# A transformer pair on one core: heads of the first mixer woven into its projections, and two edits to the expert stages

## The reference, cut to what matters

```
p = rms_norm(x) @ w_in            # columns: q,k | v | rg | mq,mk | mv | mo | i,f
y_ret = head_norm(retention(rope(q), rope(k), v)) * silu(rg)       # 4 heads, 64/128 wide
q2, k2 = silu(causal_conv(mq,mk)) # 4 taps
y_ml  = head_norm(gated_attention(q2, k2, mv, gates i and f)) * sigmoid(mo)
x = x + concat(y_ret, y_ml) @ w_out
```

```
expert = top 2 of one group per token;  out = sum_k gate_k * (silu(x @ w1[e]) * (x @ w3[e])) @ w2[e]
```

## Time and profile before

| | us |
|---|---|
| median of three runs (2335.35 to 2337.67) | 2337.12 |
| the profiled execution, its own time | 2344.5 |
| its span | 2342.7 |
| VectorE's wait for the large constants ends | 28.15 |
| first product of the mixer: start, end | 15.72, 31.7 |
| first half of the out product ends (the first out tile free) | 160.7 |
| last out product ends, embedding product begins | 175.76 |
| feed-forward stage begins | 183.6 |
| first weights of expert stage one issued | 1076.2 |
| last hidden product of stage one, of stage two | 1611.4, 2311.4 |

### The profile page before, as it was taken

The page is one execution under the profiler, slowest core; times in us unless marked ns, Lnnn a source line. Parts: engine busy times, 40 slices in busy tenths (PEclk is TensorE's granted clock), DMA queues, the critical chain, the costliest instruction groups (busy, mean ns, idle before and its releaser), DMA issues.

```text
span 2342.7 us, 20745 instructions
## 1 busy us (share of the span) xinstructions
PE 2050.2 (88%) x8573; PEld 1091.0 (47%) x8573; DVE 709.2 (30%) x1346; ACT 343.8 (15%) x725; POOL 65.2 (3%) x79
## 2 busy tenths in 40 slices
PE   7989999998999999999987778785799797887875
PEld 3557776455577764445633333332355433333331
DVE  1247465325475654023300000000764200000001
ACT  1221000214310012000100000001243100000001
POOL 0000000001000000000000000001000000000000
PEclk9979999997999999999899999998799799999998
DMA  8517667344176675112999999999211999999995
GB/s 310 184 36 262 241 216 270 130 169 144 57 267 216 245 270 168 39 72 77 368 428 427 427 427 428 427 428 396 90 56 43 375 428 426 427 429 426 428 427 229
DMA packets 154559, 639.16 MB, mean 273 GB/s; under 512 B 16600, under 2 KB 67480, under 8 KB 129760
## 3 DMA queue, kind: packets, MB, share of 16 engines
q1 hardware_dynamic: 135328, 596.04, 64.1%
q0 software_dynamic: 9824, 24.89, 3.0%
q10 hardware_dynamic: 9312, 16.88, 1.9%
HBM read 622.33 MB, written 25.30 MB: 276 GB/s over the span
## 4 chain that ended last, share of the span: by engine, by line
PE 75%; DMA 13%; issue 6%; DVE 4%; ACT 2%; POOL 0%; SPq 0%; ACTq 0%; DVEq 0%; POOLq 0%
PE psum L492 17%; PE psum L1996 16%; PE psum L934 13%; PE psum L2014 8%; PE psum L909 5%; DMA normed_t<-in_w 4%; DMA ring<-in_w 4%; PE psum L1512 4%; DMA arena<-in_w 1%; PE psum L922 1%; PE psum L1969 1%; DMA expert_inputs<-arena 1%; PE psum L478 1%; PE psum L1645 1%; PE psum L1653 1%
## 5 line engine op out<-in xcount | busy, mean ns | idle before, releaser
L492 PE MATMUL psum<-ring,normed_t 128*128 128x512 f32 (+1 forms) x864 | 355.1, 572 | 6.3 <-DVE scaled L2206 2.5
L934 PE MATMUL psum<-normed_t,ring 128*128 128x256 f32 x1408 | 305.5, 379 | 0.0
L934 PEld LDWEIGHTS psum<-normed_t,ring 128*128 128x128 f32 x1408 | 267.5, 190 | 40.6 <-issue 4.3
L492 PEld LDWEIGHTS psum<-ring,normed_t 128*128 128x128 f32 x864 | 162.1, 199 | 188.2 <-issue 185.2
L1996 PE MATMUL psum<-ring,arena 128*64 128x512 f32 x640 | 196.8, 677 | 51.9 <-issue 51.8
L1996 PE MATMUL psum<-ring,consts 128*64 128x512 f32 x640 | 188.1, 650 | 55.0 <-issue 55.0
L2305 DVE TENSOR_TENSOR scaled<-scaled,psum 128x512 f32<-128x512 f32 x32 | 22.0, 687 | 610.7 <-PE psum L1996 610.7
L839 DVE SCALAR_TENSOR_TENSOR arena<-ring,silu_c,arena 128x1024 f32<-128x1024 f32 x168 | 204.5, 1278 | 0.0
L2014 PE MATMUL psum<-ring,consts 128*64 128x512 f32 x640 | 169.8, 594 | 26.0 <-ACT consts L2144 12.5
L1996 PEld LDWEIGHTS psum<-ring,arena 128*64 128x64 f32 x640 | 65.3, 155 | 178.6 <-issue 178.6
L1996 PEld LDWEIGHTS psum<-ring,consts 128*64 128x64 f32 x640 | 62.3, 148 | 174.4 <-issue 173.8
(11 more groups left out here) (394 smaller groups left out, 2039.9 us busy)
## 6 DMA issues: line engine op xcount, KB each, us to landing
ring<-in_w SPq DMA_DIRECT2D x120, 2048.0 KB, 28.8
arena<-in_w SPq DMA_DIRECT2D x48, 2048.0 KB, 29.3
ring<-in_w_mod SPq DMA_DIRECT2D x24, 2048.0 KB, 8.7
normed_t<-in_w SPq DMA_DIRECT2D x24, 2048.0 KB, 32.8
ring<-in_ffn_w_up SPq DMA_DIRECT2D x44, 1024.0 KB, 9.6
ring<-in_ffn_w_down SPq DMA_DIRECT2D x10, 2048.0 KB, 8.7
expert_outputs<-consts ACTq DMA_DIRECT2D x64, 256.0 KB, 10.7
ring<-in_ab_w_in SPq DMA_DIRECT2D x6, 2048.0 KB, 20.4
```

Of the source, the lines that this page charges most:

```text
L492: m = te.eng.matmul(PS[:, bank, 0:n], src[:, k0 + k, P * t:P * t + P], w[:, k, :], start=(k == 0), stop=(k == kc - 1))
L934: m = pe.matmul(PS[:, b, 256 * hf:256 * hf + 256], w[:, hf, k, P * cc:P * cc + P], HT[:, k, 0:T], start=(k == 0), stop=(k == KC - 1))
```

## The change

1. The gates' tile comes third in the stream, mqk second. The gates are one product of eight rows; a small product with eight columns of the identity (`forget_rows`) moves rows 4 to 7 to a place of their own.
2. The heads of both mixers are cut into steps that `group` and `out_half` put between the projections' products: v carries the gates' second half, rg the retention, mv and mo the second mixer and the turns of the first; the out product is split into its input halves j = 0 and j = 1, so that the first half of all four results comes ahead of the last turns. Banks are dealt anew; ScalarE's and VectorE's lists follow.
3. `Experts.pe` waits for banks 0 to 3 before the picking, not for all.
4. In stage two, for pair 0, the out product goes ahead of the turn of pair 1.

```diff
-        AB_TILES = [("qk", 0, 512), ("v", 512, 512), ("rg", 1024, 512), ("mqk", 1536, 512),
-                    ("mv", 2048, 512), ("mo", 2560, 512), ("if", 3072, 8)]
+        AB_TILES = [("qk", 0, 512), ("mqk", 1536, 512), ("if", 3072, 8), ("v", 512, 512), ("rg", 1024, 512),
+                    ("mv", 2048, 512), ("mo", 2560, 512)]
...
-            for t in range(2):
-                rows(te, "ab.v", t, 2 + t, ("act", f"ab.v{t}"), last=t == 1)
-            for t in range(2):
-                rows(te, "ab.rg", t, 4 + t, ("act", f"ab.rg{t}"), last=t == 1)
...
+
+            w = te.weights("ab.if")[:, 0:64].rearrange("p (k n) -> p k n", k=8)
+            te.take(2, "act", "ab.f")
+            for k in range(KC):
+                m = pe.matmul(PS[0:8, 2, 0:256], w[:, k, :], HT[:, k, 0:T], start=(k == 0), stop=(k == KC - 1))
+            p.step(m, "ab.if.done", "ab.if.used")
...
-            for t in range(2):
-                rows(te, "ab.mv", t, 2 + t, ("dve", f"ab.mv{t}"), last=t == 1)
...
+            def group(name, t, bank, reader, steps):
+                w = te.weights(name).rearrange("p (k n) -> p k n", k=KC)
+                te.take(bank, *reader)
                 for k in range(KC):
-                    m = pe.matmul(PS[0:4, 6, 256 * j:256 * j + 256], w[:, k, 4 * j:4 * j + 4], HT[:, k, 0:T],
-                                  start=(k == 0), stop=(k == KC - 1))
-            p.step(m, "ab.if.done", "ab.if.used")
+                    for step in steps.get(k, ()):
+                        step()
+                    m = pe.matmul(PS[:, bank, :], HT[:, k, P * t:P * t + P], w[:, k, :], start=(k == 0), stop=(k == KC - 1))
+                p.step(m, f"{name}.t{t}", *([f"{name}.used"] if t else []))
+
+            def forget_rows():
+                pe.wait_ge(sems["act"], upto("act", "ab.i"))
+                p.step(pe.matmul(PS[0:4, 2, 256:512], ident[0:8, 4:8], G8, start=True, stop=True), "ab.fsel")
...
+                p.step(m, f"ab.ytr{j}{t}")
+
+            def out_half(n, t, b, j, steps):
+                w = te.weights(f"ab.out{n}").rearrange("p (k n) -> p k n", k=KC)
+                if j == 0:
+                    te.take(b, "dve", f"ab.res{n}{t}")
+                for k in range(4 * j, 4 * j + 4):
+                    for step in steps.get(k, ()):
+                        step()
+                    m = pe.matmul(PS[:, b, :], YH[:, k, P * t:P * t + P], w[:, k, :], start=(k == 0), stop=(k == KC - 1))
+                if j == 1:
+                    p.step(m, f"ab.out{n}.t{t}", *([f"ab.out{n}.used"] if t else []))
+
+            group("ab.v", 0, 3, ("act", "ab.v0"), {2: [forget_rows]})
+            group("ab.v", 1, 4, ("act", "ab.v1"), {})
+            group("ab.rg", 0, 5, ("act", "ab.rg0"), {0: [lambda: ret_scores(0), lambda: ret_scores(1)], 2: [gate_columns],
+                                                     4: [lambda: ret_values(0), lambda: ret_scores(2)],
+                                                     6: [lambda: ret_values(1), lambda: ret_scores(3)]})
+            group("ab.rg", 1, 2, ("act", "ab.rg1"), {1: [lambda: ret_values(2)], 3: [lambda: ret_values(3)]})
+            group("ab.mv", 0, 3, ("dve", "ab.mv0"), {})
+            group("ab.mv", 1, 4, ("dve", "ab.mv1"), {0: [lambda: ml_scores(0)], 4: [lambda: mixed_turn(0, 0, 5), lambda: mixed_turn(0, 1, 2)],
+                                                     6: [lambda: ml_scores(1)]})
+            group("ab.mo", 0, 5, ("act", "ab.mo0"), {2: [lambda: ml_values(0)], 3: [lambda: ml_scores(2)], 6: [lambda: ml_values(1)],
+                                                     7: [lambda: ml_scores(3)]})
+            group("ab.mo", 1, 2, ("act", "ab.mo1"), {3: [lambda: ml_values(2)], 6: [lambda: ml_values(3)]})
+            pe.wait_ge(sems["dve"], upto("dve", "ab.yt01"))
+            out_half(0, 0, 0, 0, {})
+            out_half(1, 0, 1, 0, {})
+            out_half(0, 1, 5, 0, {})
+            out_half(1, 1, 2, 0, {2: [lambda: mixed_turn(1, 0, 3)]})
+            mixed_turn(1, 1, 4)
+            pe.wait_ge(sems["dve"], upto("dve", "ab.yt10"))
+            out_half(0, 0, 0, 1, {})
+            out_half(1, 0, 1, 1, {4: [lambda: emb_turn(te, 0)]})
             pe.wait_ge(sems["dve"], upto("dve", "ab.yt11"))
-            for n in range(2):
-                for t in range(2):
-                    rows(te, f"ab.out{n}", t, 2 * n + t, ("dve", f"ab.res{n}{t}"), src=YH, last=t == 1,
-                         within={(1, 0): (0, lambda: emb_turn(te, 0)), (1, 1): (5, lambda: norm_pe(te, "n.ffn0", (0,)))}.get((n, t), (-1, None)))
+            out_half(0, 1, 5, 1, {})
+            out_half(1, 1, 2, 1, {6: [lambda: norm_pe(te, "n.ffn0", (0,))]})
...
+            for t in range(2):
+                ac.wait_ge(sems["pe"], upto("pe", f"ab.v.t{t}"))
+                p.step(ac.activation(V[:, t, :], PS[:, 3 + t, :], ACT.Copy), f"ab.v{t}")
+                if t == 0:
+                    for c in range(4):
+                        ac.wait_ge(sems["dve"], upto("dve", f"ml.conv{c}"))
+                        p.step(ac.activation(MQK[:, c, :], RTMP[:, c, :], ACT.Silu), f"ml.mqk{c}")
+            for t in range(2):
+                ac.wait_ge(sems["pe"], upto("pe", f"ab.rg.t{t}"))
+                p.step(ac.activation(SRG[:, t, :], PS[:, (5, 2)[t], :], ACT.Silu), f"ab.rg{t}")
             ac.wait_ge(sems["pe"], upto("pe", "ret.pv3"))
             p.settle()
...
+            for t in range(2):
+                ac.wait_ge(sems["pe"], upto("pe", f"ab.mo.t{t}"))
+                p.step(ac.activation(SMO[:, t, :], PS[:, (5, 2)[t], :], ACT.Sigmoid), f"ab.mo{t}")
...
+            head_norm_sums(dv, p, "ret")
+            head_norm_apply(dv, p, "ret", lambda t: PS[:, 6 + t, :], lambda t: SRG[:, t, :], lambda t: YTOK[:, t, 0:512], "ab.y0")
+            values_in(0)
+            g_max(0)
+            ml_causal(0)
+            mixer_columns(0)
+            g_max(1)
+            ml_causal(1)
+            ml_weight(0)
+            values_in(1)
+            ml_weight(1)
+            g_max(2)
+            ml_causal(2)
+            g_max(3)
+            ml_causal(3)
+            ml_weight(2)
+            ml_weight(3)
+            dv.wait_ge(sems["pe"], upto("pe", "ml.pv3"))
+            dv.wait_ge(sems["act"], upto("act", "ml.em"))
...
+            for t in range(2):
+                for n in range(2):
                     if (n, t) == (1, 1):
                         norm_columns(dv, p, "n.ffn0", (0,), lambda t: g_ffn[0])
-                        dv.wait_ge(sems["pe"], upto("pe", "ab.out1.t1"))
-                    p.step(dv.tensor_tensor(xr, xr, PS[:, 2 * n + t, :], ALU.add), f"ab.res{n}{t}")
-                    if n and on("ffn0"):
-                        norm_scale(dv, p, "n.ffn0", t)
+                    dv.wait_ge(sems["pe"], upto("pe", f"ab.out{n}.t{t}"))
+                    xr = X[:, t, 512 * n:512 * n + 512]
+                    p.step(dv.tensor_tensor(xr, xr, PS[:, ((0, 1), (5, 2))[t][n], :], ALU.add), f"ab.res{n}{t}")
+                norm_scale(dv, p, "n.ffn0", t)
...
-                for who in te.banks.values():
-                    wait(pe, *who)
+                for b in range(4):
+                    wait(pe, *te.banks[b])
+                self.pe_first(te)
                 te.banks = {}
-                self.pe_first(te)
...
@@ -2074,9 +2119,12 @@
                 for c in range(PAIRS):
                     self.pe_hidden(te, c, 0)
                     self.pe_hidden(te, c, 1)
-                    if c + 1 < PAIRS:
+                    late = self.nt == 2 and c == 0
+                    if c + 1 < PAIRS and not late:
                         self.pe_turn(te, c + 1)
                     self.pe_out(te, c)
+                    if late:
+                        self.pe_turn(te, 1)
```

More of the change, by code:

```diff
@@ L559, in ab_pe @@
-            pe.wait_ge(sems["dve"], upto("dve", "ml.rows"))
-            pe.wait_ge(consts_loaded, 16)
-            te.take(3, "dve", "ml.cols")
-            for t in range(2):
-                pe.transpose(PS[:, 3, 4 * t:4 * t + 4], gates4[:, 0 + P * t:P * t + P], ident[0:4, 0:4])
-                m = pe.transpose(PS[:, 3, 8 + 4 * t:12 + 4 * t], gates4[:, 256 + P * t:256 + P * t + P], ident[0:4, 0:4])
-            p.step(m, "ml.colt")
-            pe.wait_ge(sems["dve"], upto("dve", "ml.mqk"))
@@ new lines, in gate_columns, with ml_scores @@
+            def gate_columns():
+                pe.wait_ge(sems["dve"], upto("dve", "ml.rows"))
+                te.take(4, "dve", "ml.cols")
+                for t in range(2):
+                    pe.transpose(PS[:, 4, 4 * t:4 * t + 4], gates4[:, 0 + P * t:P * t + P], ident[0:4, 0:4])
+                    m = pe.transpose(PS[:, 4, 8 + 4 * t:12 + 4 * t], gates4[:, 256 + P * t:256 + P * t + P], ident[0:4, 0:4])
+                p.step(m, "ml.colt")
+            def ml_scores(h):
+                if h == 0:
+                    pe.wait_ge(sems["act"], upto("act", "ml.mqk3"))
+                    pe.wait_ge(consts_loaded, 16)
```

(3 more changed lines are left out.)

166 lines of the change are left out of this document (66 added, 100 removed).

## The result

| | median us | runs | profiled execution, us (span, mean clock) |
|---|---|---|---|
| before | 2337.39 | 2335.35, 2337.12, 2337.67, 2343.37 | 2344.5 (2342.7, 0.940) |
| after | 2312.34 | 2309.21, 2311.30, 2313.37, 2315.61 | 2309.21 (2307.4, 0.948) |

Ratio 0.9889, interval 0.9866 to 0.9912: 25.0 us, or 1.1%, faster. The forecast was 2305.5, in a range of 2299 to 2316. The two profiled executions differ by 35.3 us, 10 more than the medians: the one of before was 7 slower than its median, the one of after was the fastest of its four. So what follows compares stages, not whole spans.

What follows compares the result with a forecast made beforehand. TensorE's stream was taken to bound the kernel outside the expert stages, the weight stream within them; -24.5 - 2.7 - 4.5 = -31.7 us off the median 2337.1 gave 2305.4, say 2305.5, range 2299 to 2316.

Steps and rivals of the forecast that it cites:

- Mixer, -24.5: First mixer: gates, heads and out product lose TensorE time once projections fill the gaps; -24.5 us (-20.8 to -25.3).
- the switch between filler and small groups: First mixer: cost of going in and out of 18 small groups, 36 times; 0.8 us taken, bounds 0 and 4.5.
- The tightest slack, the copy of bank 4: First mixer: VectorE must copy bank 4 out (0.7 us) during two products (1.7 us) before ml values 0; slack 1.0 us.
- The cover named for it: Start of the stream: v has some 20 us for 2 MB, hiding the gates' tile; without it at most 5.7 us lost.
- Rival C: Merged first mixer: granted clock falls to 1.2 GHz for half the stream, 43 us more, 2349 us; chance 0.03.
- Rival B: First mixer: some waits come late and the clock drops once more; 3 + 3 us, 2311 to 2313; chance 0.15.
- the heads' 15.85 us at 0.54: First mixer's heads: a busy stretch at mean granted clock 0.54, claimed to be about 8.0 us at full clock.
- the 19.2: First mixer's heads: of 35.7 us, 16.5 is TensorE work at high clock; the rest goes if projections fill every gap, -19.2 us.
- Four banks, -2.7: Expert stage one: picking begins 1.7 us earlier, plus 1.0 if the shorter pause keeps the clock up; -2.7 us (0 to -4.6).
- All of the 1.7 falls into that hole: Expert stage one: the picking's 1.7 us earlier start all shortens the DMA standstill at 1140.20 to 1145.60, 4.6 us lost.
- rival A: Expert stages give nothing: the gather lands later by TensorE's gain and the weight stream only shifts its hole; 2312 us; chance 0.14.
- Out product ahead, -4.5: Expert stage two: out product ahead of turn 1 closes the DMA hole; -4.5 us with 0.2 from the four-bank edit (-2 to -4.8).

Runs made afterwards that it cites:

- the stages alone: The kernel before with the four-bank wait and stage two's out product ahead of the turn, first mixer untouched: 2335.0 us, ratio 0.9976.
- The mixer alone: The kernel after with the four-bank wait and stage two's out product order taken back: 2317.8 us, ratio 0.9912; again 2317.7 us, 0.9910.

## Why the prediction was right, and where its sizes were not

**Mixer, -24.5: right.** 23.8 in the trace. Every wait walked through had fired; the embedding product was forecast at about 151 and began at 149.77, or 152.0 without the lucky start; what is left for the switch between filler and small groups is 25.3 - 23.8 = 1.5 us and not 0.8, inside the bounds, if the other terms were exact. The tightest slack, the copy of bank 4, was 0.8 us instead of 1.0 (the copy ends at 101.25, the first values that write the bank begin at 102.07). VectorE's timeline of after:

```profile
100.56 0.69 DVE L784 COPY arena<-psum 128x512 f32<-128x512 f32 x1 [0.69 <-PE psum L532]
```

and TensorE's:

```profile
102.07 0.39 PE L586 MATMUL psum<-arena 128*128 128x129 f32 x2
```

The gates' tile took 16.6 us to land instead of 5.7; it now stands in the queue right behind the large constants and ahead of 2 MB tiles. The cover named for it held, and the gates began without a wait.

Rival C (the clock) did not come: 1.00 in all five windows above. The Trainium skill ("TensorE: Matmul & The Clock Gate", A second HAM failure mode: psum-queue depth-cycling) speaks of short idling between groups; here eight banks are cycled too, but there was no idling between them, and the clock stayed. Rival B, late waits, is out too: no row of the stretch carries one.

That the heads' 15.85 us at 0.54 would shrink to 8.0 with the clock was counted as part of the 19.2. The sum was right, but that reason is not shown: with the clock raised by dummies the heads did not get shorter. What the traces show is that other work fills them.

**Four banks, -2.7: the step that failed.** "All of the 1.7 falls into that hole" came true for that hole and not for the stage. In the 8 us from 31.4 us after the stage's first issue of arena weights, the DMA time lost is 5.0 us in the mean of six profiles with all banks and 3.3 in the eight with four, 1.7 less. What failed is the price of the gather: the prediction named it ("if turn 1 waits, the next slots come later") but left it out of the central value and gave it only the lower bound, 0.

The gather keeps its time because it waits for a DMA of its own. POOL's program lets it go only when the copy of the rows to DRAM (expert_inputs) has landed. The last write of that copy, in after:

```profile
1097.80 0.53 POOL L2398 DMA_DIRECT2D expert_inputs<-arena  x1 [0.55 <-ACT arena L2178]
```

It landed 15.9 us later, and the gather went out at 1114.62, 0.9 us behind that. So it is in all 14 profiles: the write lands after 15.0 to 16.3 us, and the gather follows by 0.9, whatever TensorE does; in stage two it is 17.7 to 19.2 and again 0.8 to 0.9. The line of VectorE that the profile names at the gather's idle time in stage one (L2288, L2347, L2352 and others) is a bystander.

With the picking earlier, the reload passes this fixed point. At a lead of 1.27 us or more the gather lands after 4.2 to 4.4 us and turn 1 waits for nothing; at 0.90 and less it lands after 10.4 to 12.8 and turn 1, where it comes first, waits 2.7 to 6.7. Then slots 4 and 5 come 6 to 11 us later, and a second hole opens by how late they are: none at 21.9 and 22.4 us behind the reload, 0.2 us at 22.9, 1.3 and 1.4 at 24.5 and 24.6, 2.5 at 25.8, 3.7 at 26.9. How late depends on the wait and on how long the clock then stays down. In the mean of the six profiles with four banks and the old order the second hole is 1.5 us, so nearly all of the 1.7 is given back; stage one shrank by 0.4 us, within its scatter. The prediction named this mechanism as rival A, with 0.14; in stage one it was the likelier case. The rows for it were there: the gather's issue 2.57 us ahead of the reload, and 2.7 us to be taken off that. That the measured 2312 is also rival A's price is a coincidence: stage two did gain, and the stages alone were worth 5.6 us.

**Out product ahead, -4.5: right mechanism, size too large.** The stage means differ by 3.0 us. The 4.3 us were read from one execution, in which the clock stayed low through the out product (9.77 us). In six profiles with the old order the wait is always there (4.9 to 6.3 us), but the out product took 7.09 in three and 9.7 to 10.0 in three, and the hole (the 8 us from 52 us after the stage's first issue of arena weights) was 0.8 to 1.5 us in the first three and 3.5 to 3.8 in the others, 2.4 in the mean. The term should have been sized from both levels.

**The sum.** By stages 23.8 + 0.4 + 3.0 = 27.2 us; timed 24 to 27. Against 31.7 the shortfall is 2.3 (banks), 1.5 (out), 0.7 (mixer), and up to 3 us that the timed runs may lack against the traces. The mixer alone lacks about as much (21 to 22 against 23.8), at the edge of its intervals. Of the ten profiled executions with the merged mixer eight are the fastest of their kernel, so a traced one is not the median one. Whether anything is lost behind the mixer, and where, stays open: only profiled executions can be looked into. That the total fell inside the range owes nothing to luck in the mixer's term, but the two stage terms, 7.2 together, were worth 3.4 by the traces.

## What to carry to other kernels

When an engine gets earlier, the DMAs that it releases get earlier too, and can pass those of another engine that keep their own time. Before counting the gain, list the issues within a few microseconds of the one that moves, ask which will now stand behind it, and what each of them waits for (here the landing of an earlier DMA). Where a term depends on whether the clock drops after a wait, take it from several executions or from both levels. Idle gaps in heads that other engines set are worth filling with real work; keeping the clock up with dummies was worth 1 to 2 us net here, real fillers more than 20.

## What the runs showed of the hardware

A gather on POOL's queue, issued 1.27 us or more ahead of the first 2 MB tiles of SyncE's reload, landed after 4.2 to 4.4 us (five profiles); issued 0.90 us ahead or later, after 10.4 to 12.8 us (nine profiles). Nothing between 0.90 and 1.27 us was measured.

A 512 KB write of rows to DRAM, issued while the weights of the stage were coming in, took 15.0 to 16.3 us to land in stage one and 17.7 to 19.2 in stage two (14 profiles).

A product on float32 operands shows as two records, 0.43 us per 512 columns each, 0.86 in all. The Trainium skill ("FP8 and Floating Point Precision", TensorE Precision Notes) gives float32 four passes; the trace shows two records, and 0.86 us is about four times 0.21 us, an estimate of what 512 columns would take at one per cycle of the 2.4 GHz level.
